# Late stage by token groups: two tiles first, the rest inside the first U and V pair phase

## What is computed

```
mixed = sigmoid(gate_a) * (a_out @ w_up_a) + sigmoid(gate_b) * (b_out @ w_up_b)
x1 = layer_norm(alpha * x + g1 * (mixed @ w_o), ln1_g, ln1_b)
h2 = x1 * (1 + sc2) + sh2
q  = (h2 @ wq).reshape(n, 8, 2, 128)
s1, s2 = q[:, :, 0] . keys1, q[:, :, 1] . keys2          # 128 keys each
t1, i1 = top_k(s1, 16);  t2, i2 = top_k(s2, 16)
top_s, pos = top_k(t1[..., :, None] + t2[..., None, :], 16)   # 8 heads x 16 = 128 experts a token
act = gelu(einsum('td,thkd->thk', h2, u_tab[idx]))
ffn = einsum('thk,thkd->td', softmax(top_s) * act, v_tab[idx])
y  = layer_norm(alpha * x1 + g2 * ffn, ln2_g, ln2_b)
```

## Time and profile before

| | |
|---|---|
| median of three runs | 2962.83 us (2947.91 to 2966.34) |
| the profiled execution | 2960.43 us |
| its span in the trace | 2958.7 us |
| PE, DVE, POOL, ACT busy | 2220.9, 1665.8, 1359.1, 240.7 us |
| moved to and from HBM | 763.01 MB read, 10.04 MB written |

### The profile page before, as it was taken

The page is one execution under the profiler, slowest core; times in us unless marked ns, Lnnn a source line. Parts: engine busy times, 40 slices in busy tenths (PEclk is TensorE's granted clock), DMA queues, the critical chain, the costliest instruction groups (busy, mean ns, idle before and its releaser), DMA issues.

```text
span 2958.7 us, 29531 instructions
## 1 busy us (share of the span) xinstructions
PE 2220.9 (75%) x9678; PEld 881.6 (30%) x9678; DVE 1665.8 (56%) x3582; ACT 240.7 (8%) x476; POOL 1359.1 (46%) x1559
## 2 busy tenths in 40 slices
PE   5999699943588898686792046777777777777998
PEld 3345355532344444342451001111111111111222
DVE  2597577545522221524279976666666667666812
ACT  1111211121010100200100000000000000000000
POOL 0243122100133322000058877777777777777755
PEclk7999889866699989798896589999999999999989
DMA  7477455425255445231079899999999999999988
GB/s 258 136 240 243 147 185 174 142 77 209 88 166 192 159 144 193 61 134 57 29 249 326 309 341 378 409 406 400 374 408 405 406 378 397 408 408 400 400 323 312
DMA packets 238547, 774.79 MB, mean 262 GB/s; under 512 B 32352, under 2 KB 34116, under 8 KB 237904
## 3 DMA queue, kind: packets, MB, share of 16 engines
q0 software_dynamic: 191008, 680.63, 62.0%
q1 hardware_dynamic: 47416, 92.54, 9.0%
HBM read 763.01 MB, written 10.04 MB: 261 GB/s over the span
## 4 chain that ended last, share of the span: by engine, by line
PE 38%; POOL 26%; DVE 14%; issue 13%; DMA 4%; POOLq 3%; ACT 2%; SPq 1%; PEldq 0%; DVEq 0%; ACTq 0%; PEld 0%
POOL arena L732 25%; PE bank L757 18%; DVE arena L2040 5%; PE bank L1172 4%; PE bank L900 3%; POOLq L710 2%; PE bank L896 2%; PE bank L1013 2%; DMA arena<-in_peer_v,arena 2%; PE bank L763 1%; SPq L560 1%; DMA arena<-in_w_ada 1%; PE bank L887 1%; PE bank L888 1%; PE bank L1206 1%
## 5 line engine op out<-in xcount | busy, mean ns | idle before, releaser
L1172 PE MATMUL bank<-arena 128*32 128x512 f32 x2048 | 894.1, 609 | 282.1 <-DMA arena<-in_peer_v,arena 277.7
L2040 DVE CUSTOM_DVE_ANT_0 arena<-arena 128x1024 f32<-128x1024 f32 x512 | 623.6, 1223 | 334.2 <-DMA arena<-in_peer_u,arena 332.5
L732 POOL DMA_INDIRECT arena<-in_peer_u,arena x520 | 568.7, 1094 | 505.4 <-DVE arena L1911 322.8
L757 PE MATMUL bank<-arena 128*128 128x8 f32 (+5 forms) x2088 | 594.3, 435 | 45.0 <-DVE arena L1756 24.0
L732 POOL DMA_INDIRECT arena<-in_peer_v,arena x520 | 513.3, 987 | 189.9 <-issue 126.9
L1172 PEld LDWEIGHTS bank<-arena 128*32 128x32 f32 x2048 | 181.3, 110 | 989.8 <-DMA arena<-in_peer_v,arena 656.8
L757 PEld LDWEIGHTS bank<-arena 128*128 128x128 f32 (+3 forms) x2088 | 313.3, 188 | 321.6 <-issue 283.7
L715 POOL DMA_DIRECT2D arena<-in_cache_v x256 | 137.3, 537 | 462.4 <-PE bank L1013 284.4
L715 POOL DMA_DIRECT2D arena<-in_cache_k x256 | 137.5, 537 | 418.5 <-issue 221.8
L763 PE MATMUL bank<-arena 128*128 128x128 f32 (+5 forms) x350 | 61.7, 312 | 237.7 <-DVE arena L1911 79.5
L1538 DVE TENSOR_TENSOR arena<-arena 128x512 f32<-128x512 f32 x256 | 175.2, 685 | 70.6 <-ACT arena L1228 51.0
(11 more groups left out here) (252 smaller groups left out, 1516.7 us busy)
## 6 DMA issues: line engine op xcount, KB each, us to landing
arena<-in_cache_k POOLq DMA_DIRECT2D x256, 256.0 KB, 3.5
arena<-in_cache_v POOLq DMA_DIRECT2D x256, 256.0 KB, 3.4
arena<-in_w_ada SPq DMA_DIRECT2D x12, 2048.0 KB, 10.2
arena<-in_w_in SPq DMA_DIRECT2D x10, 2048.0 KB, 9.4
arena<-in_peer_u,arena POOLq DMA_INDIRECT x520, 6.6
arena<-in_peer_v,arena POOLq DMA_INDIRECT x520, 6.6
arena<-in_peer_wq SPq DMA_DIRECT2D x4, 2048.0 KB, 8.0
arena<-scratch_gates SPq DMA_DIRECT2D x16, 260.0 KB, 2.8
```

The costliest lines, as they stand in the source:

```text
L732: nc.gpsimd.indirect_dma_start(gathered[:, j, :], None, tables[kind[0]][:, :], OFF(ap=index, axis=0)).then_inc(row_in[j], 16)
L757: ins = mm(out, a, b, start=i == 0, stop=i == len(pairs) - 1, **more)
L1172: ins = mm(acc[u][32 * j:32 * (j + 1), :], spread[:, token(x), :], gathered_row(("v", t, x))[:, 512 * u:512 * (u + 1)], start=x < 4, stop= ...
L2040: release(nc.vector.tensor_tensor_reduce(out=row, in0=row, in1=h2[:, t, :], scale=1.0, scalar=0.0, op0=MUL, op1=ADD, accum_out=act_of[t % ...
```

## The change

The late phases MIX, OUT, QUERY and PEER become two, NORM and LATE. Tokens are split into group 0 (tiles 0 and 1, 256 tokens) and group 1 (tiles 2, 3 and the samples, 264). A generator `stage(g, ...)` on PE and DVE, and a function on ACT, hold mix, output, norm, queries and scores of one group. `stage(0)` runs alone, ahead of the first U phase. `stage(1)` is taken a step at a time: PE makes one after each V block of tile 0 (x = 0 to 127), DVE one after each U block of tile 1, with `until(...)` giving the steps from which the output (22), the norms (50, 63, 76) and the transposes (63, 76, 90) may begin.

- Weights after the recurrence come in blocks of 1 MB through two slots `wlate`; all of them are loaded twice, once for each group: per group four blocks of w_up, four of w_o, eight of wq. A block is loaded once the block before the last was used. The first two of group 1 are issued after the last of group 0.
- Mix goes A0 to A3, B0 to B3, A4 to A7, B4 to B7. The samples' columns are a part of group 1's calls.
- The bias b_ada (and the 1 of 1 + scale) is added on PE by K=1 products in the phase before the recurrence, instead of on DVE in MIX.
- Key scores are made a head at a time, one head behind the queries. Those of tile 2 go into `ta` once tile 0's are used up; those of tile 3 and of the samples are written to DRAM (`scratch_s`) through two slots, and loaded back into `tb` and `ta` later.
- x rows come a tile at a time into one buffer `x2`; modulations of the samples, g2 and the second norm's vectors are loaded into the buffers of the first ones when these are done.
- On ACT, `stage(1)` stands between the first `ct` copy and the exponential of tile 1's gates; DVE's `gates_last(1)` moves from head 6 of tile 1's U blocks to the start of tile 2's.
- In pair phases gathers go u, u, v, v; `expert_values` takes two V blocks at a time and orders its calls by half, so that neighbouring calls have different column groups.
- `headones` moves among the lasting constants; PSUM jobs of the late stage use banks 0 to 4, `it` and `ct` bank 5.

```diff
@@ psum_jobs, gathers @@
+    late = 0
+    for name in ["keys", *late_jobs(0), *late_jobs(1)]:
+        fixed(late, name)
+        late = (late + 1) % 5
...
-        for x in range(SLOTS):
-            order += [("u", t + 1, x), ("v", t, x)]
+        for x in range(0, SLOTS, 2):
+            order += [("u", t + 1, x), ("u", t + 1, x + 1), ("v", t, x), ("v", t, x + 1)]
...
+OUT_AT = 22
+NORM_AT = (50, 63, 76)
+TURN_AT = (63, 76, 90)
@@ SP @@
+            late_weights("u0A0", "u0B0")
             sp.wait_ge(phase_end, 3 * (CHAIN + 1))
...
+            for g in range(2):
+                for q in range(3, 16):
+                    read(sp, up_job(g, q - 3))
+                    gate_rows_of(g, q)
+                    if q in (6, 10, 14):
+                        late_weights({6: f"u{g}A1", 10: f"u{g}B1", 14: f"wo{g}_0"}[q])
+                late_weights(f"wo{g}_1", f"wo{g}_2", f"wo{g}_3")
...
+                for h in range(PH):
+                    if h + 2 < PH:
+                        late_weights(f"wq{g}_{h + 2}")
...
+                    if g:
+                        for i, t in enumerate((3, NT)):
+                            n = P if t < NT else NS
+                            read(sp, f"s{t}_{h}")
+                            load(scratch_s[i, 0:n, 256 * h:256 * (h + 1)], score_rows[0:n, spills % 2, :], scores_out[spills % 2])
...
+                if g == 0:
+                    late_weights("u1A0", "u1B0")
@@ PE @@
+                for q, (br, m) in enumerate(MIXES):
...
+                    yield
+                yield from until(OUT_AT)
+                pe.wait_ge(mixed_ready, g + 1)
+                for u in range(4):
...
+                        for k in range(KD):
+                            ins = mm(o, mixed[:, k, a:a + n], w[:, k, :], start=k == 0, stop=k == KD - 1)
+                            if k == 3:
+                                yield
...
+                for u in range(2):
+                    for i in (x, x + 1):
+                        j = i % 4
+                        ins = mm(acc[u][32 * j:32 * (j + 1), :], spread[:, token(i), :], ...)
...
+                for x in range(0, SLOTS, 2):
                     expert_values(t, x)
+                    if t == 0:
+                        for now[0] in (x, x + 1):
+                            next(rest, None)
+                        if x == SLOTS - 2:
+                            for _ in rest:
+                                pass
@@ ACT @@
                 take(f"ct{t}", pairs, ...)
+                if t == 0:
+                    stage(1)
@@ DVE @@
+                for q, (br, m) in enumerate(MIXES):
+                    yield from until(q + 3)
+                    slot = (16 * g + q) % 3
+                    dve.wait_ge(sg_ready, 16 * g + q + 1)
+                    full(dve, up_job(g, q))
...
-                if t == 0 and h % 2 == 0:
-                    read(dve, f"s0_{h // 2}")
-                if t and h == 0:
-                    read(dve, f"s{t}_3")
+                if t < 3:
+                    read(dve, f"s{t}_{h}")
+                elif h == 0:
+                    dve.wait_ge(scores_in[t - 3], 16)
...
+                    if t == 2 and h == 0:
+                        side.append(gates_last(1))
...
+                        if t == 1:
+                            now[0] = x
+                            next(rest, None)
```

More of the change, by code:

```diff
@@ L97, in constants @@
     return c
-(LOAD, PROJ, FOX, SAMPLE, PRE, STATE, CHAIN, MIX, OUT, QUERY, PEER) = range(11)
+(LOAD, PROJ, FOX, SAMPLE, PRE, STATE, CHAIN, NORM, LATE) = range(9)
+GROUPS = ((0, 2 * P), (2 * P, 2 * P + NS))
+TILES = ((0, 1), (2, 3, NT))
+SPAN = 2 * P + NS
+MIXES = [(br, m) for half in range(2) for br in "AB" for m in range(4 * half, 4 * half + 4)]
 def place_buffers(buffers, limit):
@@ L686, in _ @@
+            for e in range(2):
+                sp.wait_ge(scores_out[e], 16 * PH)
+            sp.wait_ge(top_done, 2)
+            load(buf("tb"), scratch_s[0, :, :], scores_in[0])
             for i, t in enumerate((0, 1, 2, NT, 3)):
@@ L1104, in _ @@
             head_sums("var", n2)
[L1105 to L1115 removed]
+            end_phase(pe, NORM)
             pe.wait_ge(key_in, 32)
@@ new lines, in _, with done, stage, until @@
+            end_phase(dve, NORM)
+            norms = [0]
+            tick = link.tick
+            def done(n):
+                dve.wait_ge(vector_step, n)
+            def stage(g, now):
+                span = GROUPS[g][1]
+                def until(x):
+                    while now[0] < x:
+                        yield
+                if g:
+                    full(dve, f"pq0_{2 * PH - 1}")
+                for q, (br, m) in enumerate(MIXES):
[3 more added lines that the diff above has]
+                    full(dve, up_job(g, q))
+                    o = bank(up_job(g, q))[:, 0:span]
@@ L1819, in _ @@
-            end_phase(dve, OUT)
+                        link(tt(sg[:, slot, 0:span], sg[:, slot, 0:span], o, MUL))
+                        ins = tt(mixed[:, m, 0:span], mixed[:, m, 0:span], sg[:, slot, 0:span], ADD)
+                        link(ins, job=up_job(g, q))
+                    yield
+                dve.sem_inc(mixed_ready, 1)
+                dve.wait_ge(an_in, 48)
+                for u in range(4):
+                    part = slice(256 * u, 256 * (u + 1))
+                    for i, t in enumerate(TILES[g]):
+                        yield from until(OUT_AT + 2 * (len(TILES[g]) * u + i) + 4)
+                        n = P if t < NT else NS
+                        full(dve, f"wo{g}_{u}_{t}")
+                        o = bank(f"wo{g}_{u}_{t}")[0:n, 0:256]
+                        if t < NT:
+                            link(tt(x1[0:n, t, part], o, bc[0:n, 0, part], MUL), job=f"wo{g}_{u}_{t}")
+                        else:
+                            link(nc.vector.tensor_copy(x1[0:n, t, part], o), job=f"wo{g}_{u}_{t}")
+                        yield
@@ L1822, in _ @@
+            for _ in stage(0, [SLOTS]):
+                pass
             top = buf("top")
@@ L2018, in _ @@
             run(choose(0, 0), choose(0, 1))
+            now = [0]
+            rest = stage(1, now)
             for t in range(NT):
```

512 lines of the change are left out of this document (281 added, 231 removed).

## The result

The forecast was 2876 us and faster. The changed kernel takes 2973.82 us (median of 14 runs, 2963.22 to 2991.86) beside 2964.23 us of the kernel before on the same chip (14 runs): ratio 1.0046, 95% interval 1.0026 to 1.0066. That is half a per cent slower, inside the 1% that the prediction calls no change. The second dot does come 180 us sooner; all of it is given back later.

What follows compares the result with a forecast made beforehand. Gathers (DMA) were taken to bound the pair phases, behind a late dense stage with little traffic. -168 + 54 + 12 + 3 + 7 + 10 - 4 + 1 = -85 from 2960.4 gave 2876 us; range 2842 to 2918.

Steps and rivals of the forecast that it cites:

- Dense stage: Ahead of the first U phase: half-width calls cost half, weights hide; second dot from 1508.2 to 1340.4, 168 us gained.
- the rival of a load-bound first group: First group's weight blocks: 1.5 us missing in each of 16, 24 us, total 2900; chance 0.05.
- Handover: Into the second pair phase: V waits for tile 1's gates, pausing some 16 us; +10 (3 to 20).
- Step 96: First pair phase: DVE waits some 15 us for tile 2's scores, slots absorb half; +7 (0 to 15).
- First pair phase: Takes up group 1's late stage: bytes +54, norms +12, gate-row prefetch +3, top-k wait +7; +76 without the handover.
- +54 for 19.6 MB: First pair phase: DMA is full, so group 1's added loads lengthen it; bounds 49 and 84 us.
- The text's own test: Sign of a wrong forecast: the first pair phase running below 370 GB/s would mean waits, not bytes.
- PE becomes the bound: First pair phase: V doesn't overlap between full-width products, 3.7 us a step, 29 us more, total 2905; chance 0.14.
- The first rival: Ring absorbs stalls: eight slots cut terms 12, 3, 7 and 10 to 3 in all, total 2847; chance 0.15.
- The step that failed: PE in the first pair phase: paired V costs 0.9 us a block; 257 of some 400 us, hidden by DMA.
- The lengthening of issues under a full DVE: Norms in the first pair phase: gather issues on POOL of 1.17 against 1.01 us; +12 (0 to 22).
- The starving queue: 14 weight blocks in the first pair phase stall the gathers, 8.8 us each, 123 us, total 2999; chance 0.06.

Runs made afterwards that it cites:

- single V: Changed kernel with gathers u, v, u, v and V blocks taken one at a time: 2886.36 us, ratio 0.9756, where before took 2963.81 us.
- nine slots: Changed kernel with V one at a time, order u, v, u, v, and a ninth slot for gathered rows: 2873.60 us, ratio 0.9721.
- the fourth: Runs beside before at 2963.81 us: changed kernel with V one at a time 2886.36, before with pairs 3076.86, changed kernel with a ninth slot 2937.53 us.
- the first set: Four runs separating gather order from paired V calls, in the changed kernel and the kernel before; before took 3059.47 us, ratios 0.9651 to 1.0091.
- the second: Both kernels unchanged, changed kernel with extra PE products (2955.75 us), and V one at a time with a ninth slot (2873.60 us); before took 2956.64 us.

## Why the prediction was wrong

- **Dense stage: right.** Second dot forecast at 1340.4 (168 us gained), measured 1327.6 (180.6), 12.8 us early. 10.4 of these are there at the end of the mix (1239.34 for 1249.7), 6.1 of them by an earlier start (1208.82 for 1214.89 of the earlier trace rows). The weights hid, as argued: of the rival of a load-bound first group nothing shows. The first V was forecast near 1557 and came at 1546.09.
- **Handover: the pause right, its price too low.** "Some 16 us" of pause for V: the last pair ends at 1977.38, the next begins at 1993.60, 16.2 us. DVE stood 13.32 us for the exponential of the gates:

```profile
1988.99 0.29 DVE L2098 TENSOR_REDUCE arena<-arena 128x8 f32<-128x128 f32 x1 [13.32 <-ACT arena L1582]
```

  It lengthens the second pair phase, not the first. In single V that one is 23.8 us longer than the third (356.5 and 332.7; 19.0 with nine slots, 353.9 and 334.9), where +10 (3 to 20) was forecast.
- **Step 96: right.** "Some 15 us" of DVE waiting for scores were forecast; it waits 16.74, and PE pauses for V rows soon after. The term was +7; POOL waits 12.9 us for DVE's slot there:

```profile
1875.09 0.49 DVE L2004 MAX8 arena<-arena 128x8 f32<-128x128 f32 x2 [16.74 <-ACT arena L1351]
...
1885.94 3.63 PE L1289 MATMUL bank<-arena 128*32 128x512 f32 x8 [10.40 <-DMA arena<-in_peer_v,arena]
```

- **First pair phase: near in size by luck, wrong in reason.** +76 was forecast without the handover, +88.3 measured. The term "+54 for 19.6 MB" failed. It took the DMA share of 1.01 for a limit, so that any further byte would lengthen the phase. Against it, 12.8 of these MB are worth 4.5 us in single V. What the profile shows in its place is 31.7 us of longer issues, 37.5 of waits for PE's slots and 26.0 for DVE's, less 6.8 of regular gaps. The text's own test, below 370 GB/s means waits and not bytes, came true for the five stretches together (353 GB/s) and in three of the five stretches (318, 353 and 338 GB/s, 323 of 444 us). The rival *PE becomes the bound* had the step of single V exactly (3.7 us, measured 3.75). It was set aside by "0.9 us each", which is true of pairs. (The first rival's sum is 2846.4, not 2847; nothing hangs on it.)
- **The step that failed: "now two at a time go to different column groups: 0.9 us each ... Hidden, by DMA."** It asked of pairing only what it costs PE, and found a gain. What it does to the order of gathers, of dots and of slots' release was costed at nothing, in three phases, and appears in no rival. The two later phases, forecast at +6 with the handover, cost 104 us, and single V takes 86 us off the whole kernel. The profile gives two parts for each of the two: 34 us of longer issues, which stand behind a dot, and 19 us of POOL waiting for slots that PE holds. That the two V blocks of a pair are given back late could have been seen before: a gather lands in 6.6 us, V takes 1.91, and eight slots turn over in 8 x 1.28 = 10.2 us. That leaves 1.7 us as an estimate, and the wait for a second block alone is 1.24 us and the low clock another 1.5 (3.39 for 1.91).
- The lengthening of issues under a full DVE was in the text (1.17 against 1.01 us, +12), but as a matter of DVE's load in the norms. It is one of phase: with pairs DVE is less busy (223 of 379 us) than before (219 of 327), and the issues are longer.
- **The starving queue** did not come about. Loads of 1 MB landed late beside the gathers (in 1607 to 1990 medians of 15.8 us for output and 15.3 for query weights, ahead of the pair phases 5.2 and 7.5), and the chain of 1850 to 1990 has 24.4% of query weights, yet with an eighth of their bytes single V gains 4.5 us in the phase.
- The one version that reached the forecast, 2873.6 us, is the changed kernel without the part that the forecast took for a gain. Its ninth slot is worth 9 us by the profiles (spans 2868.7 and 2877.8, in different sets) and isn't told from none by the ratios (0.9721 and 0.9756, overlapping intervals), where that run expected 25 to 40 us a phase. So the forecast's time was reached, but not for the forecast's reasons: DMA bytes don't set the first pair phase. Pairs in the first pair phase alone, where PE is full, weren't tried.

## What to carry to other kernels

When the order of work on a saturated stream is changed, cost what the new order does to the issuing engine and to how long each buffer is held, not only what it saves on the engine that consumes. Compare with the latency that the ring has to spare, here 1.7 us of 10.2. A steady state in which two engines have fallen into step can be worth 10% (here 34 us of issues on 339) and is invisible in busy shares; read it from the starts and ends of single instructions. A DMA share near 1 doesn't say that more bytes cost time: take bytes away and look.

## What the runs showed of the hardware that was not expected

- A gather's issue on POOL that begins in a DVE dot of two 128x1024 inputs ends 0.81 us after the dot (203 of 230 within 0.02 us); outside of one it takes 0.94 us. Of the 131 above 1.3 us 126 end within 0.02 us of that mark.
- The DMA share reads 0.95 and 0.96 in phases that move 349 and 351 GB/s, and 1.02 in those that move 403. It hardly sinks when the engines are not fed.
- PE's granted clock fell from 0.99 to 0.67 when V's 1.9 us of work in every 2.56 us became bursts of two blocks, 1.9 us of work at full clock in some 6 us (four gathers of 1.5). With the order of pairs but V one at a time it was 0.90. Two more products a pair brought it to 0.92, and only 15 us with it.
- In two of five sets the kernel before took 3059 and 3073 us, 3.2 and 3.7% more than in the fourth, while single V took 2954 and 2971 for 2886 (2.4 and 2.9%), and pairs in the kernel before hardly changed (3087 and 3092 for 3077). Single V also had more long issues there (35 and 33 of 256 for 14 and 7). That would fit a step that is lost there, which kernels with pairs don't have to lose; but the kernel before wasn't profiled in those sets, and what disturbed them stays open. It is no fixed property of a chip: the first set (3059 us) and the second (2957) carry the same chip number, 15 minutes apart. The Trainium skill, Perfetto Trace Analysis (Roofline), gives 358 GB/s for each of two cores that share a memory and up to 435 for one alone; whether a neighbour was at work no run here shows.
